# All sixteen gate chunks as split products, the recurrence's scan in four parts, attention outputs kept by ScalarE

## The chip, the cores and the metric

The kernel runs on one core of a Trainium2 chip. The metric is the device time of one launch in microseconds (us). Engines are named TensorE (PE; its weight loads are PEld), VectorE (DVE), ScalarE (ACT), GpSimd (POOL) and SyncE (SP, which issues most DMAs).

## What is computed

One inference step of a two-layer encoder, for 256 new prompt tokens and 32 sample tokens, 288 token columns in all, width 1024. The reference, cut to one layer:

```
z = x @ w_in                      # columns: [rnn 1024 | q 1024 | k 128 | v 128 | rnn gate 1024 | attn gate 1024]
q, k = rope(z_q), rope(z_k)       # 16 query heads, 2 key/value heads of 64
g_rnn, g_attn = sigmoid(z_gr), sigmoid(z_ga)
u  = causal depthwise conv (width 4) of z_rnn
gx = sigmoid(u @ w_x + b_x); ga = sigmoid(u @ w_a + b_a)      # 16 blocks of 64
a  = exp(-8 * ga * softplus(-a_param)); b = sqrt(1 - a*a) * gx * u
h_t = a_t * h_(t-1) + b_t                                     # the recurrence, over the tokens
o  = attention of q over its own and the two previous chunks of 64 tokens, with a sink per head
m  = g_rnn * (h @ w_br_rnn) + g_attn * (o @ w_br_attn)
x  = layernorm(alpha * x + m @ w_out)
x  = layernorm(alpha * x + shared_expert(x) + top-8-of-64 experts(x))
```

All data are float32.

## The kernel before, in words

Activations lie transposed, features on the 128 partitions and 288 tokens along the free axis (`xT`, eight chunks of 128 features). A weight matrix comes in **pieces** of 1024 x 256 (1 MB), one DMA each, into a ring of three slots (`dense`). The list `PIECES` gives their order: four for the rnn stream, one for k and v, four for q (`D_Q` = 5), eight for the gates (`D_G` = 9), eight for the two branches, four for `w_out`, and the rest. SyncE loads piece d when piece d-3 has been used.

A piece gives two output **chunks** of 128 columns, and TensorE makes a chunk in one of two ways:

- `over_features` (L569): eight plain float32 products, which the profile records as 16 MATMULs;
- `over_parts` (L582 to L584): weight and activation are each split into a high and a low part of type float32r, and three products (high x high, high x low, low x high) are made for each of eight feature chunks: 24 MATMULs. For this ScalarE copies the piece to its high part (`high_parts`, L1069, two instructions of 128x1024 for a piece) and VectorE subtracts to get the low part (`low_parts`, L1409, two instructions). The list `SPLIT` names the pieces that are split; a piece's place in it is called f here. The high part has two buffers, so piece f waits until piece f-2 has been used.

Each engine has its program written out by hand, and they wait for each other's semaphores only. The stretch that matters here is the attention stage of each layer. It has, on TensorE, in this order (L702 to L799): sixteen gate chunks in five places ahead of and between the attention steps, set by the tables

```
GATES_AHEAD = ((0, 1), (2, 3), (4,))
GATES_WITH = ((5, 6), (7,), (8,), (9, 10), (11,), (12, 13), (14,), (15,))
```

1. The projection of q: eight chunks, each followed by the two gate products of the recurrence (L695), whose sigmoids ScalarE writes (L1153), while VectorE rotates q (L1504 to L1507).
2. Gate chunk 0; two transposes of k (L722) and the 32 sample tokens' scores (L734, L735); gate chunk 1.
3. Transposes of the sample tokens' probabilities (L743, L744), which wait for VectorE to normalise them (L1534); scores of pair 0 (`pair_scores`, L713, L714); gate chunks 2 and 3.
4. Output of the sample tokens (L756, L757), which waits until ScalarE has copied the transposed probabilities (L1188, L1189; semaphore `s_pT_kept`); gate chunks 4, 5 and 6.
5. The loop over the eight **pairs** c of heads: scores of pair c+1, gate chunk(s) of `GATES_WITH[c]`, output of pair c-1 (`pair_output`, L771 to L773), transposes of pair c's probabilities (L791). Afterwards the output of pair 7, one transpose of the states (L799), and the branch products (L582 to L584 again).

Chunk m of the gates is written to bank m % 2 of PSUM, and ScalarE applies a tanh and keeps it (`keep_gates`, L1162); chunk m+2 waits for that. In `bank_of` gate chunk 0 waits until all of the recurrence's gate products in even banks have been read.

Beside this, VectorE has for pair c: `mask_and_max(c)` (L1562 to L1526: adds the mask to the scores, takes the row maxima) when the scores are there; `normalise` (L1531 to L1534) when ScalarE has made the exponentials (L1203); `keep_output` (L1587), a copy of the pair's output out of PSUM; and `low_parts` in the turns that `LOW_WITH` names. ScalarE has the exponentials, two copies of the transposed probabilities (L1224, L1225), the gates, and `high_parts` in the turns of `HIGH_WITH`.

The **recurrence** runs beside it: ScalarE computes the decay a (L1177, eight instructions) and a tanh (L1182, eight), VectorE computes the squares (L1553, L1554, four pairs), ScalarE a square root (L1193), and VectorE multiplies and scans all eight feature chunks in one block (L1573 to L1579), after `mask_and_max(0)` and ahead of `normalise` of pair 0. From the scan come a high part by ScalarE (L1214, at pair `H_WITH` = 2) and a low part by VectorE (L1598, L1599, one pair later).

After the attention stage come the branch products, `w_out`, a layer norm, the router, and sixteen rounds over four experts each. In the first of these, between the experts' first products (`up`, L910) and `turn` (L920), the shared expert's second product is made (`shared_down`, L871, eight chunks in two banks); VectorE adds each chunk to the residual (L1792), and TensorE waits for the last of these before it goes on. VectorE makes the one-hot table of the next four experts (`one_hot`, L1722) after them.

## Time and profile before

| | us |
|---|---|
| median of 3 runs | 1590.09 (1589.77 to 1591.45) |
| the profiled execution, its own time | 1589.3 |
| its span, first to last instruction | 1587.5 |
| TensorE busy | 1550.0 (98% of the span) |
| VectorE busy | 741.5 (47%) |
| ScalarE busy | 573.9 (36%) |
| attention stage of a layer (TensorE's gate chunk 0 to the transpose of the states) | 90.2 |

TensorE is busy in nearly all of the span, and the chain of work that ended last runs over it for 92% of the time. A busy share is an average: matmuls overlap, and inside the attention stage the three engines wait for each other for fractions of a microsecond. The two layers have the same timeline, shifted by 783.32 us; where the text reads a time of the second layer, the first layer's is that much earlier.

### The profile page before, as it was taken

The page shows a single profiled execution, that of the slowest core. Times are in us where ns is not written, and L with a number is a line of the kernel's source. Part 1 is how long each engine was busy: PE and PEld are TensorE (multiplying, and loading weights), DVE is VectorE, ACT ScalarE, POOL GpSimd, SP SyncE. Part 2 cuts the span into 40 slices and gives each one's busy share as a digit, 9 for nine tenths or more (in the row PEclk, how much of TensorE's full clock was granted, in tenths as well). Part 3 has the DMA queues.
Part 4 walks back from the last instruction along what each step waited for, and adds up shares of the span by engine and source line. Part 5 has one row for each costly group of instructions (what it writes and reads, how often), then busy time and mean ns, then how long its engine had stood idle before and what let it go on. Part 6 is the DMA issues. An engine that isn't in the chain of part 4 may idle for free.

```text
span 1587.5 us, 25312 instructions
## 1 busy us (share of the span) xinstructions
PE 1550.0 (98%) x9446; PEld 1034.5 (65%) x9446; DVE 741.5 (47%) x1513; ACT 573.9 (36%) x1108; POOL 25.0 (2%) x40
## 2 busy tenths in 40 slices
PE   7999999999999999999999999999999999999996
PEld 7968997655655565555598699975565555556554
DVE  5768667332433333233474776562243333324335
ACT  5756433222232232223267664342223223222322
POOL 2000000000000000000010000000000000000000
PEclk9999999999999999999999999999999999999998
DMA  8552446599999999999546424458999999999991
GB/s 235 188 209 85 134 160 245 212 372 409 410 399 402 401 417 401 403 404 402 206 127 232 153 91 153 147 212 322 401 404 398 408 404 416 400 404 407 401 407 45
DMA packets 141557, 477.38 MB, mean 301 GB/s; under 512 B 10020, under 2 KB 74084, under 8 KB 108724
## 3 DMA queue, kind: packets, MB, share of 16 engines
q1 hardware_dynamic: 139728, 473.50, 77.0%
q0 software_dynamic: 1408, 2.85, 0.7%
q8 instruction: 44, 0.72, 0.2%
q10 hardware_dynamic: 356, 0.13, 0.0%
q14 instruction: 21, 0.17, 0.0%
HBM read 474.88 MB, written 1.57 MB: 300 GB/s over the span
## 4 chain that ended last, share of the span: by engine, by line
PE 92%; DVE 5%; ACT 2%; issue 1%; DMA 0%; SPq 0%; DVEq 0%; ACTq 0%
PE ps L910 28%; PE ps L933 14%; PE ps L582 6%; PE ps L583 6%; PE ps L584 6%; PE ps L569 6%; PE ps L954 4%; PE ps L955 4%; PE ps L893 4%; PE ps L892 4%; PE ps L895 2%; PE ps L942 1%; PE ps L871 1%; PE ps L920 1%; PE ps L1004 1%
## 5 line engine op out<-in xcount | busy, mean ns | idle before, releaser
L910 PE MATMUL ps<-experts,xg 128*64 128x512 f32 x2048 | 445.0, 592 | 0.0
L910 PEld LDWEIGHTS ps<-experts,xg 128*64 128x64 f32 x2048 | 146.9, 137 | 291.5 <-issue 290.6
L582 PE MATMUL ps<-parts 128*128 128x288 f32 x768 | 232.4, 303 | 1.1 <-DVE dense_lo L1409 0.4
L933 PE MATMUL ps<-experts,hid 128*64 128x512 f32 x1024 | 226.8, 595 | 0.4 <-ACT hid L1283 0.4
L584 PE MATMUL ps<-parts,dense_lo 128*128 128x288 f32 x768 | 226.1, 294 | 0.0
L1749 DVE SCALAR_TENSOR_TENSOR yl<-ps,gsl,yh 128x512 fp32r<-128x512 f32 x128 | 96.1, 751 | 254.8 <-ACT yh L1291 254.8
L1737 DVE TENSOR_TENSOR hid<-ps,hid 128x256 f32<-128x256 f32 x64 | 27.2, 425 | 378.6 <-ACT hid L1278 378.6
L1278 ACT ACTIVATE hid<-ps 128x256 f32<-128x256 f32 x64 | 24.6, 385 | 404.8 <-PE ps L910 404.8
L933 PEld LDWEIGHTS ps<-experts,hid 128*64 128x64 f32 x1024 | 71.6, 137 | 131.9 <-issue 127.9
L1270 ACT ACTIVATE xg<-ps,gperm_all 128x256 f32<-128x256 f32 x256 | 130.8, 562 | 71.5 <-PE ps L895 71.5
L582 PEld LDWEIGHTS ps<-parts 128*128 128x128 f32 x768 | 144.3, 188 | 4.8 <-issue 2.3
L584 PEld LDWEIGHTS ps<-parts,dense_lo 128*128 128x128 f32 x768 | 144.5, 188 | 0.0
L892 PE MATMUL ps<-oh,xh 128*128 128x256 f32 x512 | 136.4, 288 | 0.0
L1291 ACT ACTIVATE yh<-ps,gsl 128x512 fp32r<-128x512 f32 x128 | 88.1, 688 | 128.8 <-PE ps L933 128.8
L893 PE MATMUL ps<-oh,xl 128*128 128x256 f32 x512 | 133.5, 282 | 0.0
L954 PE MATMUL ps<-ohT,yh 128*128 128x288 f32 x480 | 132.2, 305 | 0.0
L955 PE MATMUL ps<-ohT,yl 128*128 128x288 f32 x480 | 129.1, 295 | 0.0
L1409 DVE TENSOR_TENSOR dense_lo<-dense,parts 128x1024 fp32r<-128x1024 f32 x96 | 113.2, 1221 | 19.4 <-ACT parts L1069 19.4
L569 PE MATMUL ps<-xT,dense 128*128 128x288 f32 x448 | 112.6, 409 | 4.4 <-ACT B L1153 2.7
L1756 DVE TENSOR_TENSOR ffT<-ps,ffT 128x288 f32<-128x288 f32 x240 | 109.6, 456 | 15.4
L583 PE MATMUL ps<-parts 128*128 128x288 f32 x384 | 113.3, 295 | 0.0
L1069 ACT ACTIVATE parts<-dense 128x1024 fp32r<-128x1024 f32 x96 | 96.1, 1052 | 42.3 <-PE ps L584 41.7
(287 smaller groups left out, 1964.0 us busy)
## 6 DMA issues: line engine op xcount, KB each, us to landing
experts<-in_w SPq DMA_DIRECT2D x384, 1024.0 KB, 10.0
dense<-in_w_in SPq DMA_DIRECT2D x34, 1024.0 KB, 5.5
dense<-in_w_br_rnn SPq DMA_DIRECT2D x8, 1024.0 KB, 5.3
dense<-in_w_br_attn SPq DMA_DIRECT2D x8, 1024.0 KB, 5.2
dense<-in_w_out SPq DMA_DIRECT2D x8, 1024.0 KB, 5.2
dense<-in_ws SPq DMA_DIRECT2D x6, 1024.0 KB, 5.5
tok<-in_x_prompt SPq DMA_DIRECT2D x1, 1024.0 KB, 5.7
out_y_prompt<-tok SPq DMA_DIRECT2D x2, 512.0 KB, 2.6
```

The costliest lines, as they stand in the source:

```text
L569: last = mm(bank[:, 0:n], w[:, k, col:col + P], rhs(k), start=k == 0, stop=k == KC - 1)
L582: mm(bank[:, 0:T], w_hi[:, k, col:col + P], hi[:, k, :], start=k == 0, stop=False)
L583: mm(bank[:, 0:T], w_hi[:, k, col:col + P], lo[:, k, :], start=False, stop=False)
L584: last = mm(bank[:, 0:T], w_lo[:, k, col:col + P], hi[:, k, :], start=False, stop=k == KC - 1)
L892: mm(o, xh[:, t, x], oh[:, t, :], start=t == 0, stop=False)
L893: mm(o, xl[:, t, x], oh[:, t, :], start=False, stop=False)
L910: last = mm(ps[e % 2 * CAP:(e % 2 + 1) * CAP, UP[u], :], xg[:, k, e * CAP:e * CAP + CAP], experts[:, e, 0:2, k * DE:k * DE + DE], start=k ...
L933: last = mm(ps[e % 2 * CAP:(e % 2 + 1) * CAP, DOWN[u][b], :], hidT[:, u, m, e % 2 * CAP:(e % 2 + 1) * CAP], experts[:, e, 2, m * D + b * 5 ...
L954: mm(o, yh[:, u, c * P:c * P + P], ohT[:, u, :], start=u == 0, stop=False)
L955: last = mm(o, yl[:, u, c * P:c * P + P], ohT[:, u, :], start=False, stop=u == 1)
L1270: last = activation(xg[:, k, :], ps[:, SWAP[j], k % 2 * 256:k % 2 * 256 + 256], ACT.Identity, bias=gperm_all[:, L, 1, k:k + 1], scale=gper ...
L1409: V.tensor_tensor(low[:, x], slot[:, x], as_f(whi[:, f % 2, x]), ALU.subtract).then_inc(wlo_ready, 1)
```

## The change

- **Split.** The gate pieces that were not split (the first four, gate chunks 0 to 7) join `SPLIT`. Their high and low parts are made in two new turns of the q projection (after q chunks 5 and 7), and at two new places (`F_G - 2`, `F_G - 1`) between that and the pairs.
- **Order of the gates.** `GATES_AHEAD` becomes ((0, 1, 2), (3,), (4,)). ScalarE keeps chunk 0 ahead of the sample tokens' exponentials, chunk 1 behind them. Gate chunk 0 waits only for the read of the product that last used its bank. The last gate chunk, 15, is made in two halves of four feature chunks, one ahead of pair 6's output, one ahead of pair 7's.
- **Recurrence.** The multiply and scan are made for two feature chunks at a time: part 0 where the whole stood, parts 1 to 3 in the turns of pairs 0 to 2. The high part of h is made one pair later (`H_WITH` = 3), and so is the low part.
- **Outputs.** `keep_output` moves from VectorE to ScalarE.
- **Shared expert.** TensorE goes on with `turn` and the transposes of the gate table before it waits for VectorE's last addition, and VectorE makes the next one-hot table ahead of the additions.

```diff
-SPLIT = list(range(D_IN + 1, D_KV + 1)) + list(range(D_Q, D_G)) + list(range(D_G + 4, D_ROUTER))
+SPLIT = list(range(D_IN + 1, D_KV + 1)) + list(range(D_Q, D_ROUTER))
-GATES_AHEAD = ((0, 1), (2, 3), (4,))
+GATES_AHEAD = ((0, 1, 2), (3,), (4,))
-H_WITH = 2
+H_WITH = 3
...
-                elif i >= Z_GATE:
+                elif i == Z_GATE:
+
+                    pe.wait_ge(z_free[i % 2], z_count(L, Z_GATE - Z_GATE % Z_DEEP) + 1)
+                elif i > Z_GATE:
                     pe.wait_ge(z_free[i % 2], z_count(L, i))
...
+                def last_gate(ks):
+                    m = 2 * KC - 1
+                    if ks[0] == 0:
+                        bank_of(L, Z_GATE + m)
+                    return over_parts(L, ps[:, z_bank(Z_GATE + m), :], D_G + m // 2, m % 2 * P, x_hi, x_lo, ks=ks)
+
...
-                    if c > 0:
+                    if c == KC - 1:
+                        last_gate(range(KC // 2))
+                        pair_output(c - 1)
+                    elif c > 0:
...
+                last_gate(range(KC // 2, KC)).then_inc(z_ready[(2 * KC - 1) % 2], 1)
                 pair_output(KC - 1)
...
-                    if c in (1, 3):
+                    if c % 2:
                         high_parts(L, F_Q + 2 + c // 2)
...
+                act.wait_ge(xc_used, L + 1)
+                keep_gates(GATES_AHEAD[0][:1])
                 act.wait_ge(s_max, L * (KC + 1) + 1)
...
+                keep_gates(GATES_AHEAD[0][1:2])
+                high_parts(L, F_G - 2)
                 act.wait_ge(gxu, L + 1)
...
                 keep_gates(GATES_AHEAD[1])
+                high_parts(L, F_G - 1)
                 act.wait_ge(m2_ready, (L + 1) * (KC // 2))
...
+                def keep_output(c):
+                    act.wait_ge(s_o, L * (KC + 1) + c + 2)
+                    activation(qT[:, c, 0:TP], ps[:, 6, 0:TP], ACT.Copy).then_inc(o_ready, 1)
...
+                    if 0 < c < KC - 1:
+                        keep_gates(GATES_WITH[c])
                     if c > 0:
-                        keep_gates(GATES_WITH[c])
+                        keep_output(c - 1)
...
+                def recurrence(j):
+                    x, c = slice(2 * j * U, 2 * (j + 1) * U), slice(2 * j, 2 * j + 2)
+                    dve.wait_ge(mult_ready, L + 1)
+                    link(V.memset(gl_[:, c, 0:1], 1.0))
+                    V.memset(a_[:, c, 0:1], 0.0)
+                    V.memset(a_[:, c, US - 1:US], 0.0)
+                    link(V.tensor_tensor(gxF[:, x], gxF[:, x], glF[:, x], ALU.mult))
+                    link(V.tensor_copy(gx_[:, c, US - 1:US], h0[:, c, :]))
+                    V.tensor_tensor_scan(glF[:, x], aF[:, x], gxF[:, x], 0.0, ALU.mult, ALU.add).then_inc(h_scan, 1)
...
+                recurrence(0)
...
                     if c == 0:
                         mask_and_max(1)
-                    if c > 0:
-                        keep_output(c - 1)
+                    if c < 3:
+                        recurrence(c + 1)
+                    if c == 2:
+                        last_states()
                     if c in LOW_WITH:
                         low_parts(L, F_G + LOW_WITH.index(c))
...
                     slots_to_tokens(n, 1)
+                    if after:
+                        after()
...
                     hidden(q, 0)
                     hidden(q, 1)
+                    dve.wait_ge(og_ready, q + 1)
+                    one_hot(q + 1, 1)
```

Three places show the new order; line numbers in the rows of the change are its own. First, ScalarE from the last q chunk (rows `tmp<-ps`) to the copy of the sample tokens' probabilities (`PTa<-ps`), before:

```order
L1153 ACTIVATE B<-ps,prm_all 128x291 [waits z_free0,z_ready0]
L1153 ACTIVATE B<-ps,prm_all 128x291 [waits z_free1,z_ready1]
L1169 ACT_TABLE_LOAD
L1169 ACTIVATE S,ats<-ps,ats 128x160 [waits s_max]
L1169 ACTIVATE S,ats<-ps,ats 128x160 x3
L1171 ACTIVATE ats<-ats 128x4
L1177 ACTIVATE B<-B,c 128x291 [waits z_free1,decay_set,z_free0,gxu]
L1177 ACTIVATE B<-B,c 128x291 x7
L1162 ACTIVATE B<-ps 128x288 [waits z_ready0,xc_used]
L1162 ACTIVATE B<-ps 128x288 [waits z_ready1]
L1182 ACTIVATE B<-B,c 128x291 [waits act_own]
L1182 ACTIVATE B<-B,c 128x291 x7
L1188 ACTIVATE PTa<-ps 128x256 [waits s_pT]
```

and in the change:

```order
L1081 ACTIVATE parts<-dense 128x1024 [waits z_ready1,dense_in1]
L1081 ACTIVATE parts<-dense 128x1024
L1174 ACTIVATE B<-ps 128x288 [waits z_ready0,xc_used]
L1183 ACT_TABLE_LOAD
L1183 ACTIVATE S,ats<-ps,ats 128x160 [waits s_max]
L1183 ACTIVATE S,ats<-ps,ats 128x160 x3
L1185 ACTIVATE ats<-ats 128x4
L1174 ACTIVATE B<-ps 128x288 [waits z_ready1]
L1081 ACTIVATE parts<-dense 128x1024 [waits z_ready1,dense_in2]
L1081 ACTIVATE parts<-dense 128x1024
L1193 ACTIVATE B<-B,c 128x291 [waits z_free1,decay_set,z_free0,gxu]
L1193 ACTIVATE B<-B,c 128x291 x7
```

Two copies to a high part (`parts<-dense`, L1069 before and L1081 now, two instructions each) stand ahead of the decays and the tanhs, which are followed by the same copy to `PTa`.

Second, VectorE from the mask of pair 2 (`S<-ps,cst`) to the mask of pair 3, before:

```order
L1562 TENSOR_TENSOR S<-ps,cst 128x384 [waits s_pT,s_scores]
L1562 TENSOR_TENSOR S<-ps,cst 128x384
L1565 TENSOR_REDUCE ats<-S 128x2 [waits s_masked]
...
L1534 TENSOR_SCALAR S<-S,ats 128x128 x2
L1587 COPY qT<-ps 128x256 [waits s_o]
L1409 TENSOR_TENSOR dense_lo<-dense,parts 128x1024 [waits whi_ready] x2
L1562 TENSOR_TENSOR S<-ps,cst 128x384 [waits s_pT,s_scores]
```

and in the change:

```order
L1588 TENSOR_TENSOR S<-ps,cst 128x384 [waits s_pT,s_scores]
L1588 TENSOR_TENSOR S<-ps,cst 128x384
L1591 TENSOR_REDUCE ats<-S 128x2 [waits s_masked]
...
L1559 TENSOR_SCALAR S<-S,ats 128x128 x2
L1603 MEMSET B 128x2 [waits mult_ready]
L1604 MEMSET B 128x2 [waits dve_own]
L1605 MEMSET B 128x2
L1606 TENSOR_TENSOR B<-B 128x582
L1607 COPY B<-prm_all 128x2 [waits dve_own]
L1608 SCALAR_TENSOR_TENSOR B<-B 128x582 [waits dve_own]
L1434 TENSOR_TENSOR dense_lo<-dense,parts 128x1024 [waits whi_ready] x2
L1588 TENSOR_TENSOR S<-ps,cst 128x384 [waits s_pT,s_scores]
```

The copy out of PSUM is gone and a part of the recurrence (six instructions; its scan is the row `SCALAR_TENSOR_TENSOR B<-B 128x582`) stands ahead of the low parts.

Third, VectorE at the shared expert, from the experts' hidden values (`hid<-ps,hid`) on, in the change:

```order
L1765 TENSOR_TENSOR hid<-ps,hid 128x256 [waits silu_done]
L1746 ISA [waits og_ready]
L1750 TENSOR_TENSOR oh<-cst,rank 128x768 [waits xg_full]
L1822 SCALAR_TENSOR_TENSOR ffT<-xT,ps 128x288 [waits z_ready0]
L1822 SCALAR_TENSOR_TENSOR ffT<-xT,ps 128x288 [waits z_ready1]
```

The one-hot table (`oh`) stood behind the eight additions (`ffT<-xT,ps`, L1792 before) and now stands ahead of them.

## Rows read from the trace of the kernel before

**Rows 1.** TensorE's waits, second layer's attention stage: total us, times, longest

```profile
PE ps L569 <- ACT B L1153: 1.4, 1, 1.4
PE ps L743 <- DVE S L1534: 1.3, 1, 1.3
PE ps L771 <- ACT PTa L1225: 1.0, 1, 1.0
PE ps L569 <- ACT B L1162: 0.7, 1, 0.7
PE ps L791 <- DVE S L1534: 0.5, 1, 0.5
```

**Rows 2.** Chain in order of time, same stage: start us, us, what

```profile
887.58 0.36 PE ps L756 x2
...
890.46 11.84 PE ps L569 x48
902.30 0.64 PE ps L713 x4
...
923.28 0.33 PE ps L582
...
926.67 0.65 PE ps L791 x6
...
932.65 0.81 PE ps L791 x6
```

**Rows 3.** Branch products: us, busy (instructions) of PE PEld DVE ACT POOL, PEclk, DMA, GB/s

```profile
177.00:245.00 68.00, 68.00 (x516) 67.95 (x515) 42.15 (x62) 24.70 (x30) 3.00 (x5) 1.00 0.45 145
```

**Rows 4.** ScalarE, timeline, second layer: start us, us, instruction [idle before, releaser]

```profile
873.11 0.39 ACT L1169 ACTIVATE S<-ps,ats 128x160 f32<-128x160 f32 x1 [5.32 <-DVE ats L1526]
...
875.61 3.54 ACT L1177 ACTIVATE B<-B,c 128x291 f32<-128x291 f32 x8 [0.80 <-DVE B L1548]
...
879.63 3.53 ACT L1182 ACTIVATE B<-B,c 128x291 f32<-128x291 f32 x8
...
884.12 0.38 ACT L1162 ACTIVATE B<-ps 128x288 f32<-128x288 f32 x1
...
908.53 2.00 ACT L1069 ACTIVATE parts<-dense 128x1024 fp32r<-128x1024 f32 x2
```

**Rows 5.** VectorE, timeline, second layer's attention stage

```profile
891.56 0.07 DVE L1573 MEMSET B<- 128x8 f32 x1 [1.86 <-ACT B L1193]
...
894.51 5.01 DVE L1579 TENSOR_TENSOR_SCAN B<-B 128x2328 f32<-128x2328 f32 x1
...
903.22 1.02 DVE L1562 TENSOR_TENSOR S<-ps,cst 128x384 f32<-128x384 f32 x2 [1.76 <-PE ps L714]
...
905.81 1.02 DVE L1562 TENSOR_TENSOR S<-ps,cst 128x384 f32<-128x384 f32 x2
...
908.80 1.01 DVE L1534 TENSOR_SCALAR S<-S,ats 128x256 f32<-128x256 f32 x4
...
910.76 2.35 DVE L1409 TENSOR_TENSOR dense_lo<-dense,parts 128x1024 fp32r<-128x1024 f32 x2
...
922.12 2.28 DVE L1598 TENSOR_TENSOR h_lo<-B,parts 128x2048 fp32r<-128x2048 f32 x1
```

**Rows 6.** VectorE, timeline, first layer, q projection: the sinks' tables

```profile
76.94 1.38 DVE L1400 COPY sinkS<-sinkP 32x4 f32<-32x4 f32 x8
```

**Rows 7.** Chain in order of time, first layer, shared expert

```profile
299.80 7.97 PE ps L871 x32
...
308.49 0.65 PE ps L920 x4
```

**Rows 8.** VectorE, timeline, first layer, shared expert

```profile
308.43 0.96 DVE L1722 TENSOR_TENSOR oh<-cst,rank 128x768 fp32r<-128x768 f32 x1 [0.19 <-DVE ffT L1792]
```

**Rows 9.** Stretches at the end of the program, columns as in rows 3

```profile
1575.00:1577.00 2.00, 0.28 (x2) 0.00 (x0) 1.51 (x8) 1.08 (x3) 0.00 (x0) 1.00 0.00 0
1577.00:1578.00 1.00, 0.00 (x0) 0.00 (x0) 0.96 (x3) 1.00 (x2) 0.00 (x0) 0.80 0.00 0
```

More of the change, by code:

```diff
@@ L570, in over_features, with over_parts @@
                 return last
-            def over_parts(L, bank, d, col, hi, lo, ready=None):
+            def over_parts(L, bank, d, col, hi, lo, ready=None, ks=range(KC)):
                 f = SPLIT.index(d)
@@ L576, in over_parts @@
                 w_lo = dense_lo[:, d % RING, :].rearrange("p (k c) -> p k c", k=KC)
-                for k in range(KC):
+                for k in ks:
                     if col == 0 and k % 4 == 0:
@@ L872, in shared_down, with shared_added @@
                         last.then_inc(z_ready[c % 2], 1)
+                def shared_added():
                     for b in range(2):
@@ L956, in combine, with quad @@
                         last.then_inc(c_full, 1)
-                def quad(n, first=False, last=False):
+                def quad(n, first=False, last=False, after=None):
                     if not first:
@@ L976, in round_of @@
                         meanwhile()
-                    quad(q, first=True)
+                    quad(q, first=True, after=shared_added if meanwhile else None)
                     with pe.Fori(1, NQUAD - 1) as i:
@@ L1225, in _ @@
                     activation(PTa[:, w, 1, :], ps[:, 5, 0:3 * P], ACT.Copy).then_inc(s_pT_kept, 1)
+                    if c == KC - 1:
+                        keep_gates(GATES_WITH[c])
                     if c in HIGH_WITH:
                         high_parts(L, F_G + HIGH_WITH.index(c))
+                keep_output(KC - 1)
                 act.wait_ge(o_ready, (L + 1) * (KC + 1))
@@ L1514, in _ @@
                         sink_tables()
-                    if c in (1, 3):
+                    if c > 0 and c % 2:
                         low_parts(L, F_Q + 2 + c // 2)
@@ L1603, in _ @@
                         mask_and_max(1)
-                    if c > 0:
-                        keep_output(c - 1)
+                    if c < 3:
+                        recurrence(c + 1)
+                    if c == 2:
+                        last_states()
                     if c in LOW_WITH:
                         low_parts(L, F_G + LOW_WITH.index(c))
-                keep_output(KC - 1)
                 low_parts(L, F_BR + 1)
@@ L1756, in add_output, with quad @@
                         V.tensor_tensor(ffT[:, c, :], ps[:, SWAP[c % len(SWAP)], 0:T], ffT[:, c, :], ALU.add).then_inc(c_added, 1)
-                def quad(n, i, first=False, last=False, hidden_made=False):
-                    if not last:
+                def quad(n, i, first=False, last=False, made=False):
+                    if not last and not made:
                         dve.wait_ge(og_ready, n + 1)
                         one_hot(n + 1, i + 1)
-                    if not hidden_made:
+                    if not made:
                         hidden(n, 0)
@@ L1805, in round_of @@
                         meanwhile()
-                    quad(q, 0, first=True, hidden_made=first)
+                    quad(q, 0, first=True, made=first)
                     with dve.Fori(1, NQUAD - 1) as i:
```

31 lines of the change are left out of this document (9 added, 22 removed).

## Prediction

> **What bounds the kernel now.** I read the busy shares first: TensorE is busy for 98% of the span, VectorE for 47%, ScalarE for 36% (the table of the profile). That says only that TensorE's own work or a wait of TensorE has to shrink; whether the other two engines have room is a question of where, not of their average. The second view is TensorE's waits inside the attention stage, the one stage that the change rebuilds: 1.4, 1.3, 1.0, 0.7 and 0.5 us, all for ScalarE or VectorE [rows 1]. That is 4.9 us a layer. These are idle times from the modelled end of the last matmul; the next one could have started some 0.2 us before that end, so the first, second and fourth cost about 4.1 us together and not 3.4. The third view is the order of time around these waits, on TensorE [rows 2], ScalarE [rows 4] and VectorE [rows 5].
>
> I work in the second layer's times. The median of the runs is 1590.1 us, the profiled execution 1589.3 us; I sum against the latter and add the same difference to the median.
>
> **Gate chunks.** A plain chunk costs 11.84 / 3 = 3.95 us [rows 2]. A split chunk in a row of them costs 24 x 68.00 / 516 = 3.16 us [rows 3]; alone between other work, from its first product to the next kind, 926.67 - 923.28 = 3.39 us [rows 2]. Of the eight chunks that change, five stand first in their group and three behind another: 5 x 3.39 + 3 x 3.16 = 26.4 us against 31.6, a gain of 5.2 us a layer. Chunk 15 in two halves pays the 0.2 us of a start once more. If all old waits went too, a layer would win 5.2 - 0.2 + some 5.5. The price is 4 more high parts of 2.00 us on ScalarE [rows 4] and 4 more low parts of 2.35 us on VectorE [rows 5], and the recurrence in the midst of the pairs. The rest is about whether these are covered.
>
> **Up to the pairs: 5.4 us earlier.** ScalarE ended its q work at 866.5; a table load and 5.32 us of idle time followed, to 873.11 [rows 4]. The high part behind q chunk 5 lies in its idle time. The one behind q chunk 7 lasts until 868.5, VectorE's low part of its second half (1.2) until 869.7; two small copies later VectorE takes the sample scores, at 870.2, where it was 871.6, so the exponentials start at 871.7 instead of 873.1. They last 1.7 (873.11 to 875.61 less the wait of 0.80); keeping chunk 1 takes 0.4, the next high part 2.0: 875.8. Then decays 3.4, chunk 2 0.4, tanhs 3.4, copies of the probabilities 1.1: they are out at 884.2, which is where they are now (884.12 is the instruction behind them [rows 4]). The 1.4 us won ahead of the exponentials and the 0.8 us wait for VectorE are eaten by 2.0 us of high part.
>
> TensorE comes earlier. It reached the sample output at 887.58 [rows 2]. Without the three waits (4.1) and with chunks 0 to 3 split (15.8 becomes 13.3, so 2.5) it is there at 881.0. So **a wait of 3.2 us for ScalarE stands where none was**; the output starts at 884.2, 3.4 us earlier than before. Chunks 4 to 6 take 3.39 + 2 x 3.16 = 9.7 instead of 11.84 us. Call the start of pair 1's scores T: it was 902.3 and becomes 896.9.
>
> **The pairs: 5.5 us later.** VectorE's steps from row to row: a mask with its maxima 905.81 - 903.22 = 2.6; a normalisation 1.35 (1.01 and its two small predecessors); low parts 2.3, their first half 1.2; the recurrence's block lasted 899.52 - 891.56 = 7.96 us, so a quarter is 2.0, plus four instructions' fixed time and links again, 2.5 [rows 5]. The bounds of this last price are 2.0 (nothing fixed) and 2.7; I take 2.5, because every one of its six instructions is issued four times. The mask of pair 1 starts 0.9 us behind T. Then, in VectorE's order, recurrence 2.5, mask 2.6, normalisation 1.35, recurrence 2.5, first half of the low part for chunk 8 1.2: chunk 8 can start at T + 13.7. TensorE's own work up to there is short: a pair's turn with one chunk takes 932.65 - 926.67 = 6.0 us [rows 2], so it stands there at T + 8.7, and **waits 5.0 us** in two pieces, ahead of pair 1's transposes (about 2.4) and of chunk 8 (about 1.9), with 0.6 in small change. The second half of the low part, a mask and a normalisation end at T + 18.9, where TensorE is at T + 18.2: 0.7 more. With pair 3 there are two chunks in the turn and nothing waits. With pair 4 the low part of h (2.28 [rows 5] and a small second part, some 2.6) now falls into a turn with one chunk: mask, h, normalisation are 6.6 us behind the 0.9 of the scores, TensorE's own way 5.2: 2.3 more. Together 8.0 us. Off come the old waits of 0.5 and 1.0 and two small ones (2.0), chunk 7's 0.6, and on goes the half chunk's 0.2: plus 5.5 us.
>
> `keep_output` on ScalarE takes 0.35 us off VectorE per pair and adds 0.4 to ScalarE, whose turns have room; its cover is ScalarE's wait for the next maxima, and if it is gone it costs its 0.4 in each of eight turns. Only behind the last pair does it show: half chunk, high part, output and the high part of o now follow each other on ScalarE, and o's low part ends some 0.15 us after TensorE has finished the first two branch chunks; 0.15 a layer. DMAs keep their number; each gate piece is asked for when the piece three before it is used, at least 8 us ahead of its high part, so none is late.
>
> **First layer.** It has the sinks' tables on VectorE, 2 us, of which [rows 6] shows the longest part, just ahead of the first new low part. That makes the rotation of q chunk 6, the last sigmoids and all behind them later; I follow it through to T as 1.25 us.
>
> **Shared expert.** TensorE could go on 0.7 us earlier (307.77 to 308.49 [rows 7]), and another 0.25, as a product can follow ahead of the modelled end. But the one-hot table, 0.96 us [rows 8], now stands ahead of the additions that free the two banks, and holds the third chunk for 0.5: minus 0.45 a layer.
>
> **Sum.** Second layer -5.4 + 5.5 = +0.1; first +0.1 + 1.25 = +1.35; branches +0.3; shared -0.9: **+0.9 us**, 1590.2 for the execution profiled, **1591.0** as a median. Differences within 0.2% (3.2 us) are what a measurement of this kernel can't tell from none.
>
> **Rivals.**
>
> *The cover holds.* For it speaks that in the attention stage of 90 us ScalarE and VectorE are not full. If my VectorE chains are too long by half of each wait I found (11.2 us a layer, so 5.6), the time is about 1580; chance 0.19. If no wait is left, old or new, both layers give 10.5 and the shared expert 0.9: about 1569; chance 0.08. Against it: each engine's order is fixed, and the three waits of 3.2, 5.0 and 2.3 follow from rows added up.
>
> *The clock falls* (the slower side). No wait inside the kernel is longer than 1.4 us now, and the granted clock is 1.00 throughout. After the program's last matmuls (0.28 us of them in 1575 to 1577) it reads 0.80 in the microsecond from 1577 [rows 9], so in that microsecond it left its upper level of 2.4 GHz for 1.2 GHz, with TensorE idle. My forecast has TensorE idle for 3.2 us at one place and for 2.4 and 1.9 with little between them at another. Each fall costs between nothing and a whole chunk made at half speed (3.4); the middle, 1.7, once or twice in each layer, gives +3 to +6: 1594 to 1597. It decides if the level changes at one of these waits, with TensorE as the bound behind it. Chance 0.20. The Trainium skill ("TensorE: Matmul & The Clock Gate", Part 1: The HAM clock gate) says that the throttled state is the default and activity releases it; by that rule each new long wait is followed by slow products, +3 to +6 as above, and the trace agrees for the end of the program [rows 9].
>
> *ScalarE is later still.* Its chain from 866.5 to 884.2 has no slack left. If each high part ends 0.5 us later than I think, or the decays wait, T moves by 1 to 1.5 us in both layers: 1594. Chance 0.08.
>
> **Chances.** The forecast has 0.45, nearly all within 0.2%. Faster by more than 0.2%: 0.27 of the first rival and a little of the forecast's edge, 0.31 in all. Slower: the two others and the other edge, 0.31. Same: 0.38. The range takes in the half-covered case and the clock's: 1580 to 1597; the forecast's own is 1588 to 1594.
>
> **What would show it.** Right: no plain gate chunks, split chunks at 3.2 to 3.4 us; a wait of about 3 us of TensorE for the copies of the sample tokens' probabilities; waits of about 2 us for pair 1's normalisation, for chunk 8's low part and for pair 4's normalisation; the wait for the last sigmoid (1.4) gone. Wrong: if VectorE's recurrence parts lie in its idle time and chunk 8 does not wait, the first rival holds; if the granted clock is under 1.00 inside the attention stage, the second.

## The result

The change is slower: 1599.42 us (1599.16 to 1599.82) against 1589.93 us (1588.79 to 1591.45) for the kernel before on the same chip, ratio 1.0059, 95% interval 1.0043 to 1.0075. The forecast was 1591.0, the range ended at 1597. One execution of a later kernel (the change with eight chunks plain) took 1767.9 us at a mean granted clock of 0.847 and stands in none of the comparisons.

The head of the profile of the change:

```profile
span 1597.3 us, 25646 instructions
...
PE 1553.9 (97%) x9574; PEld 1049.7 (66%) x9574; DVE 757.1 (47%) x1549; ACT 593.1 (37%) x1140; POOL 24.9 (2%) x40
```

TensorE has more busy time than before (1550.0), although the 16 gate chunks that are now split, eight in each layer, should have saved it 10.4 us. TensorE's waits in the second layer's attention stage (total us, times, longest us) answer to [rows 1]:

```profile
PE ps L798 <- DVE S L1559: 4.6, 2, 2.4
PE ps L754 <- ACT PTa L1204: 3.0, 1, 3.0
PE ps L585 <- DVE dense_lo L1434: 0.8, 1, 0.8
PE ps L711 <- DVE S L1588: 0.3, 1, 0.3
```

The old waits are gone, and the four that I had forecast stand there: 3.0 us for the copies of the sample tokens' probabilities (3.2 forecast), two of at most 2.4 for the normalisations of pairs 1 and 4 (2.4 and 2.3), and one for chunk 8's low part, of 0.8 where I had 1.9. So far the forecast holds. The chain of waits in order of time, second layer, shows what doesn't (start us, us, what); it answers to [rows 2]:

```profile
887.48 0.26 ACT PTa L1203
887.75 0.27 ACT PTa L1204
888.02 0.14 issue
888.15 0.57 PE ps L754 x2
888.72 0.61 PE ps L755 x2
...
892.42 0.61 PE ps L755 x2
893.04 0.54 PE ps L585
893.58 0.24 PE ps L586
893.82 0.24 PE ps L587
...
898.14 0.24 PE ps L587
898.38 0.24 PE ps L585
898.75 0.14 PE ps L587
```

Two products of the sample tokens' output took 0.36 us before [rows 2] and take 0.61 here; a product of chunk 4 takes 0.24 us, from 898.75 on one takes 0.14. The granted clock in the same stretches (the columns are us; PE, PEld, DVE, ACT and POOL busy; PEclk, the granted clock; DMA share; GB/s):

```profile
884.00:888.00 4.00, 1.18 (x9) 0.95 (x8) 3.42 (x5) 4.00 (x12) 0.00 (x0) 1.00 0.34 93
888.00:892.00 4.00, 3.85 (x13) 1.90 (x14) 3.86 (x6) 3.97 (x6) 0.00 (x0) 0.53 1.08 400
892.00:896.00 4.00, 4.00 (x16) 3.34 (x16) 3.80 (x13) 2.94 (x2) 0.00 (x0) 0.50 0.74 295
896.00:900.00 4.00, 4.00 (x23) 4.00 (x23) 2.47 (x4) 1.08 (x4) 0.00 (x0) 0.69 0.01 3
...
912.00:916.00 4.00, 1.55 (x16) 1.31 (x15) 3.73 (x16) 3.60 (x12) 0.00 (x0) 0.94 0.80 241
916.00:920.00 4.00, 3.23 (x16) 2.47 (x15) 3.93 (x6) 3.18 (x6) 0.00 (x0) 0.50 0.07 21
...
940.00:944.00 4.00, 1.81 (x15) 1.24 (x10) 3.93 (x10) 1.27 (x7) 0.00 (x0) 0.86 0.76 261
944.00:948.00 4.00, 4.00 (x25) 3.62 (x25) 3.09 (x7) 2.77 (x4) 0.00 (x0) 0.72 0.00 1
```

0.50 is the lower of the clock's two levels, 1.2 of 2.4 GHz. In the 4 us that hold the long waits TensorE was busy for 1.18, 1.55 and 1.81 us, and the clock fell in them or at their end. In the first layer the sample output starts at 101.53 us, and the clock falls later, in the midst of it, with TensorE busy:

```profile
100.00:104.00 4.00, 2.47 (x13) 1.25 (x13) 3.83 (x6) 3.98 (x9) 0.00 (x0) 0.90 0.99 337
104.00:108.00 4.00, 4.00 (x16) 3.34 (x16) 3.93 (x6) 3.97 (x3) 0.00 (x0) 0.50 1.03 409
```

Before the change no stretch inside the kernel is under 1.00. Over the whole stages (the same columns, first and second layer):

```profile
80.00:178.00 98.00, 88.15 (x690) 78.72 (x689) 75.18 (x179) 66.47 (x171) 1.07 (x2) 0.93 0.39 131
...
858.00:957.00 99.00, 90.23 (x671) 81.04 (x670) 73.69 (x167) 66.17 (x165) 1.07 (x2) 0.90 0.43 147
```

A mean of 0.93 over 98 us is (1 - 0.93) x 98 / 0.5 = 14 us at the lower level, 0.90 over 99 us is 20 us: 34 us in all.

For the experiments I use two lengths (us) of each layer's attention stage, from TensorE's own starts in the profiled execution: A, from the recurrence's last gate products to pair 1's scores, and B, from there to the transpose of the states. "Falls" is the number of times that the granted clock fell there, in A + in B. First layer / second layer:

| kernel | A | B | falls |
|---|---|---|---|
| before | 38.8 / 38.8 | 54.0 / 54.0 | none |
| forecast (sum) | 34.6 / 33.4 | 59.5 / 59.5 | none |
| the change | 37.4 / 37.5 | 60.4 / 61.4 | 1+2 / 1+2 |
| all four waits filled | 34.5 / 33.1 | 58.9 / 58.8 | none |
| first wait filled | 34.5 / 34.6 | 60.4 / 60.4 | 0+1 / 1+1 |
| copies moved | 32.9 / 31.5 | 61.0 / 59.5 | 0+2 / none |
| recurrence together | 37.4 / 37.5 | 56.7 / 52.9 | 1+1 / 1+0 |
| change, eight chunks plain | 34.9 / 34.9 | 60.2 / 58.8 | 0+1 / none |
| rearranged | 32.9 / 31.5 | 52.9 / 53.0 | none |
| rearranged, eight chunks plain | 34.9 / 34.9 | 52.2 / 52.2 | none |
| two parts in pair 3's turn | 31.4 / 30.1 | 54.0 / 54.0 | none |
| spread | 31.4 / 30.1 | 51.9 / 51.9 | none |

### The profile page after: what moved, and what is told of

Read it like the earlier page. It is cut to its first block, busy times and chain, and to the rows that moved or that the text cites. A ratio compares the mean times of both kernels' runs of the same rounds, so it can differ in the third digit from the quotient of the medians.

```text
span 1597.3 us, 25646 instructions
## 1 busy us (share of the span) xinstructions
PE 1553.9 (97%) x9574; PEld 1049.7 (66%) x9574; DVE 757.1 (47%) x1549; ACT 593.1 (37%) x1140; POOL 24.9 (2%) x40
## 4 chain that ended last, share of the span: by engine, by line
PE 89%; DVE 6%; ACT 3%; issue 1%; DMA 0%; SPq 0%; DVEq 0%; ACTq 0%
PE ps L920 28%; PE ps L943 14%; PE ps L585 6%; PE ps L586 6%; PE ps L587 6%; PE ps L964 4%; PE ps L965 4%; PE ps L902 4%; PE ps L903 4%; PE ps L572 2%; PE ps L905 2%; PE ps L952 1%; PE ps L879 1%; PE ps L930 1%; DVE dense_lo L1434 1%
## 5 line engine op out<-in xcount | busy, mean ns | idle before, releaser
L585 PE MATMUL ps<-parts 128*128 128x288 f32 x896 | 275.3, 307 | 2.5 <-DVE dense_lo L1434 1.7
L587 PE MATMUL ps<-parts,dense_lo 128*128 128x288 f32 x896 | 266.6, 298 | 0.0
L585 PEld LDWEIGHTS ps<-parts 128*128 128x128 f32 x896 | 171.5, 191 | 8.3 <-issue 4.2
L587 PEld LDWEIGHTS ps<-parts,dense_lo 128*128 128x128 f32 x896 | 171.6, 192 | 0.0
L586 PE MATMUL ps<-parts 128*128 128x288 f32 x512 | 154.2, 301 | 0.0
L1434 DVE TENSOR_TENSOR dense_lo<-dense,parts 128x1024 fp32r<-128x1024 f32 x112 | 132.1, 1220 | 28.0 <-ACT parts L1081 27.9
L1081 ACT ACTIVATE parts<-dense 128x1024 fp32r<-128x1024 f32 x112 | 112.1, 1051 | 40.0 <-PE ps L587 39.7
L964 PEld LDWEIGHTS ps<-ohT,yh 128*128 128x128 f32 x480 | 90.2, 188 | 24.3 <-issue 24.3
```

The source lines that it names most:

```text
L585: mm(bank[:, 0:T], w_hi[:, k, col:col + P], hi[:, k, :], start=k == 0, stop=False)
L586: mm(bank[:, 0:T], w_hi[:, k, col:col + P], lo[:, k, :], start=False, stop=False)
L587: last = mm(bank[:, 0:T], w_lo[:, k, col:col + P], hi[:, k, :], start=False, stop=k == KC - 1)
L964: mm(o, yh[:, u, c * P:c * P + P], ohT[:, u, :], start=u == 0, stop=False)
L1081: activation(whi[:, f % 2, x], dense[:, d % RING, x], ACT.Copy).then_inc(whi_ready, 1)
L1434: V.tensor_tensor(low[:, x], slot[:, x], as_f(whi[:, f % 2, x]), ALU.subtract).then_inc(wlo_ready, 1)
```

## The experiments

Theory 1: the waits end where my sum put them, and what is over it is the clock, falling behind three of them in each layer. Theory 2, its rival: the waits and the chains of ScalarE and VectorE behind them cost the time themselves, and slow products only fill time that would have been idle. The eleven kernels ran in three sets; beside each set the kernel before had a median of 1590.04, 1589.47 and 1589.52 us.

Medians hold one thing more than A and B. The first 32 records of plain products in the program (timeline of TensorE: start us, us; first the kernel before, then the change with all waits filled) take

```profile
12.19 8.00 PE L569 MATMUL ps<-xT,dense 128*128 128x288 f32 x32 [0.16 <-ACT xT L1059]
12.16 9.82 PE L572 MATMUL ps<-xT,dense 128*128 128x288 f32 x32
```

8.00 us in six of the thirteen profiles and 9.7 to 10.4 us in the other seven, because the first seven to ten of them start 0.48 us apart instead of 0.24. This lies ahead of everything that the change touches, and it moves an execution by some 2 us. So where medians of a few executions differ by 2 us or less, the lengths of the profiles' stages decide.

### The waits filled with products

```diff
+            def fill_wait(n):
+                for _ in range(n):
+                    mm(ps[:, 7, 256:512], ident, cst[:, 0:256], start=True, stop=True)
...
+                fill_wait(6)
                 pe.wait_ge(s_pT_kept, L * (KC + 1) + 1)
...
+                    if c in (1, 4):
+                        fill_wait(5)
                     pe.wait_ge(s_norm, n + 1)
```

and `fill_wait(3)` ahead of chunk 8.

> The change, with products that nothing reads put on TensorE ahead of its long waits: six ahead of the sample tokens' output, five ahead of the transposes of pairs 1 and 4, three ahead of gate chunk 8. Theory 1 (the clock): the profile of the change shows the granted clock at 0.50 to 0.53 in 888 to 896 and at 0.50 in 916 to 920, each time behind a wait of 2 to 3 us; with TensorE occupied in these waits the granted clock stays at 1.00 in the attention stages, the waits keep their ends, and the time falls from 1599.4 to about 1591 (1590 to 1593), which is what my sum gave without the clock. Theory 2 (the waits alone): the time is set by the chains of ScalarE and VectorE, the slow products only fill idle time; then it stays at 1598 to 1600, or gets longer by what the extra products overrun.

1588.07 us (1587.2 to 1590.88), ratio 0.9987 [0.9978, 0.9995]: 11.35 us less than the change, by adding work, and 2 us under the band that I had given. A and B together are 11.5 us shorter; the two profiled executions differ by 9.3 us only, as the start of the program took 2.2 us longer in this one. TensorE at the first wait, timeline, second layer:

```profile
882.70 2.75 PE L642 MATMUL ps<-cst 128*128 128x256 f32 x12
885.84 0.40 PE L760 MATMUL ps<-PTa,vc_all 128*64 128x128 f32 x2 [0.39 <-ACT PTa L1214]
```

and the stretches from there, and around pair 1's transposes:

```profile
884.00:888.00 4.00, 3.61 (x20) 2.10 (x18) 3.83 (x6) 3.98 (x10) 0.00 (x0) 1.00 0.96 313
888.00:892.00 4.00, 4.00 (x30) 3.66 (x30) 3.93 (x6) 3.97 (x3) 0.00 (x0) 1.00 1.03 410
...
908.00:912.00 4.00, 3.66 (x23) 2.43 (x21) 3.87 (x11) 4.00 (x13) 0.00 (x0) 1.00 0.39 134
912.00:916.00 4.00, 3.83 (x30) 3.69 (x32) 3.83 (x11) 0.56 (x2) 0.00 (x0) 1.00 0.02 4
```

Six products that nothing reads (twelve records) last 2.75 us, and the output starts when ScalarE is done, as without them: 19.75 us behind the last gate product here, 19.74 in the change. The clock stays at 1.00 in both stages. Theory 2 is out: the waits end where they did, and the time fell with the clock's falls.

One wait filled alone, `fill_wait(6)` ahead of the sample tokens' output:

> The change with products that nothing reads in one of the long waits alone: six ahead of the sample tokens' output. From the profiles of the change and of the run with all four places filled: up to pair 1's scores these differ by 2.9 us in the first layer and 4.4 in the second, from there to the transpose of the states by 1.5 and 2.6. If each fall of the clock has its own price, this run keeps the first saving and not the second: 1599.4 - 7.3 = 1592.1, with the granted clock still at 0.50 behind the waits of pairs 1 and 4. If a fall kept away early only lets TensorE run into a longer wait later, it stays over 1596.

1592.94 us (1592.24 to 1594.81), ratio 1.0023 [1.0013, 1.0033], against 1592.1 expected: a wait later in the stage does not take the saving back. That the number meets so closely is in part luck, for the falls were not the expected ones. Behind pair 1's wait of 2.4 us the clock did not fall in either layer (B is 60.4 in both, 1.0 less than in the change's second layer), and in the second layer it fell in spite of the filling (stretches as above):

```profile
884.00:888.00 4.00, 3.62 (x20) 1.89 (x18) 3.83 (x6) 3.98 (x9) 0.00 (x0) 1.00 1.04 368
888.00:892.00 4.00, 4.00 (x20) 3.96 (x19) 3.97 (x6) 3.96 (x3) 0.00 (x0) 0.57 1.01 401
```

It is a short fall, and A is 34.6 there for 33.1 with none. So six products do not keep the clock in every execution; why here and not in the run before is open.

### One move on ScalarE, and what a fall costs

ScalarE's four copies of the sample tokens' probabilities are put ahead of its eight tanhs:

```diff
-                act.wait_ge(act_own, (L + 1) * KC)
-                for c in range(KC):
-                    activation(gl_[:, c, :], gl_[:, c, :], ACT.Tanh, scale=c8[:, 1, L, c:c + 1]).then_inc(a_and_t, 1)
                 act.wait_ge(s_pT, L * (KC + 1) + 1)
...
                 last.then_inc(s_pT_kept, 1)
+                act.wait_ge(act_own, (L + 1) * KC)
+                for c in range(KC):
+                    activation(gl_[:, c, :], gl_[:, c, :], ACT.Tanh, scale=c8[:, 1, L, c:c + 1]).then_inc(a_and_t, 1)
```

> The change with one thing moved: ScalarE copies the sample tokens' probabilities (1.1 us) ahead of the eight tanhs (3.55 us) instead of behind them. The wait of 3 us ahead of the sample tokens' output goes, and with it the first fall of the clock; pair 1's scores come some 7 us earlier. The tanhs, the squares, the square root and the scan end 1.1 us later than now, so pair 0's transposes wait about 2 us for their normalisation and pairs 1 and 4 wait as long as in the change or longer, and the clock falls there: 1588 to 1593. If the waits in the pairs grow by all that is won ahead of them: 1597 or more.

1590.56 us (1588.86 to 1592.3), ratio 1.0003 [0.9994, 1.0012], in the middle of the band; A is 4.5 and 6.0 us shorter than in the change where I had expected some 7. Its two layers have the same waits ahead of the transposes, and the clock fell in the first layer only. TensorE at pair 1's transposes and at chunk 8, timeline, first layer:

```profile
125.79 1.54 PE L798 MATMUL ps<-cst,S 128*128 128x128 f32 x6 [2.44 <-DVE S L1559]
129.44 0.37 PE L585 MATMUL ps<-parts 128*128 128x288 f32 x1 [0.52 <-DVE dense_lo L1434]
```

and the granted clock there:

```profile
122.00:126.00 4.00, 1.49 (x14) 1.12 (x14) 3.72 (x17) 3.60 (x10) 0.00 (x0) 0.93 0.66 193
126.00:130.00 4.00, 3.48 (x18) 2.73 (x18) 3.93 (x5) 3.59 (x9) 0.00 (x0) 0.64 0.20 69
```

and second layer:

```profile
908.43 0.87 PE L798 MATMUL ps<-cst,S 128*128 128x128 f32 x6 [2.45 <-DVE S L1559]
912.08 0.37 PE L585 MATMUL ps<-parts 128*128 128x288 f32 x1 [1.92 <-DVE dense_lo L1434]
```

and its clock:

```profile
905.00:909.00 4.00, 1.55 (x17) 1.31 (x17) 3.72 (x16) 3.60 (x12) 0.00 (x0) 1.00 0.75 233
909.00:913.00 4.00, 2.08 (x18) 1.73 (x17) 3.93 (x6) 3.24 (x7) 0.00 (x0) 1.00 0.09 29
```

Two things are to be read here. The same wait of 2.44 us is followed by the lower level in one layer and by the upper in the other. And this fall costs nothing: chunk 8 starts 3.65 us behind the first transpose in both layers, since the slow transposes (1.54 us for 0.87) only shorten the next wait from 1.92 to 0.52. The first layer's second fall, at pair 4, has no wait behind it, and B is 61.0 against 59.5 there: 1.5 us. The same price stands in two other lines of the table, 60.4 against 58.8 (one fall in B, first wait filled) and 60.2 against 58.8 (eight chunks plain).

### The recurrence in one piece again

```diff
-                recurrence(0)
+                for j in range(4):
+                    recurrence(j)
+                last_states()
...
-                    if c < 3:
-                        recurrence(c + 1)
-                    if c == 2:
-                        last_states()
```

and `H_WITH` = 2.

> The change with the recurrence in one piece again (its four parts behind each other where part 0 stands, h's parts one pair earlier); all gate chunks stay split. VectorE is idle from 902.5 to 906 in the profile of the change and free in the pairs' turns then. Theory 1: the waits of 2.4 us at pairs 1 and 4 go and with them the second and third fall of the clock, the first stays: some 6 to 7 us less in each layer, 1585 to 1588. Rival: the scan in one piece delays pair 0's normalisation and so its transposes by what it wins later: 1597 to 1601.

1588.95 us (1587.15 to 1590.71), ratio 0.9989 [0.998, 0.9997]: a little over the band, 10.5 us under the change. In the second layer B falls to 52.9, with one wait of 1.4 us left for pair 0's normalisation and no fall. In the first layer, whose chain is later by the sinks' tables, that wait is 2.87 us, and the clock does fall (timeline of TensorE):

```profile
124.10 1.54 PE L798 MATMUL ps<-cst,S 128*128 128x128 f32 x6 [2.87 <-DVE S L1559]
```

So the rival's mechanism (pair 0 delayed) is there, but even with the clock it costs B 2.7 us in the first layer (56.7 for 54.0 before) and gains 1 in the second; the four parts of the change cost 6.4 and 7.4. The recurrence in one piece together with the moved copies was not run.

### Was it the split?

The first eight gate chunks are made as plain products again, in the change:

```diff
-SPLIT = list(range(D_IN + 1, D_KV + 1)) + list(range(D_Q, D_ROUTER))
+SPLIT = list(range(D_IN + 1, D_KV + 1)) + list(range(D_Q, D_G)) + list(range(D_G + 4, D_ROUTER))
...
-                high_parts(L, F_G - 2)
...
-                high_parts(L, F_G - 1)
```

> The change with the first eight gate chunks as plain products and without their four pieces' parts. ScalarE's chain to the sample tokens' probabilities is 2.0 us shorter, TensorE's way there 2.5 us longer: that wait and its fall of the clock go. The waits of the pairs stay, since the recurrence's parts do. Second layer: up to pair 1's scores 34.7 us (before 38.8, now 37.5), from there to the transpose of the states 54.0 + 5.5 + 0.6 = 60.1; so +2.1 against before, +3 in the first; less 1.1 at the shared expert: 1594. If the split was what cost the time: back to 1590 or less. If it carried its 5.2 us a layer in the change: 1603 or more.

1593.55 us (1591.2 to 1597.76, eleven executions), ratio 1.0028 [1.0018, 1.0037]: 1594 was expected. So the rest of the change loses time without any split: A is 3.9 us shorter in each layer than before, B 6.3 and 4.9 longer. The split in that order loses 5.9 us more. In the stages of the profiles it is 7.9: 5.2 in A, by the first wait that the split makes and the clock behind it, and 2.8 in B, nearly all in the second layer, where the clock fell twice instead of not at all. Its waits of 1.9 and 2.2 us at pairs 1 and 4 had one fall in the first layer, none in the second; the executions with a mean granted clock of 0.992 and 0.993 took 1597.1 to 1597.8 us, those at 0.995 and 0.996 1591.2 to 1594.1.

### The shared expert alone

The kernel before with the two edits at the shared expert:

```diff
+                def shared_added():
                     for b in range(2):
                         pe.wait_ge(z_free[b], z_count(L, Z_SH2 + KC))
...
                     slots_to_tokens(n, 1)
+                    if after:
+                        after()
...
                     hidden(q, 1)
+                    dve.wait_ge(og_ready, q + 1)
+                    one_hot(q + 1, 1)
```

> The kernel before with the change's part at the shared expert alone. By my sum minus 0.45 us a layer, so 0.9 us in all: 1589.0. If the wait was hidden anyway: no change, 1589.9. The profile of the change (from the shared expert's products to the end of the program) lets me expect 1.1 to 1.2.

1588.51 us (1587.24 to 1592.06), ratio 0.9991 [0.9982, 0.9999]. TensorE, chain in order of time, first layer:

```profile
299.50 2.14 PE ps L871 x8
301.68 6.09 PE ps L871 x24
307.76 0.44 PE ps L922 x4
```

The transposes follow the last product at once, where 0.7 us of wait stood [rows 7]. From the first product to the transposes it is 8.26 us for 8.69, my 0.45; from one layer's shared expert to the next layer's, and from the second to the end of the program, the profiles differ by 0.54 and 0.57 us, 1.1 in all. The medians differ by 1.5.

### The same work in another order

If theory 1 holds, the order of ScalarE and VectorE decides, not their load. TensorE's order is untouched; ScalarE's copies stand ahead of the tanhs, pair 0's mask ahead of the squares, and:

```diff
-H_WITH = 3
+H_WITH = 4
...
-                    if c == 0:
-                        mask_and_max(1)
-                    if c < 3:
-                        recurrence(c + 1)
-                    if c == 2:
+                    if c in (0, 2, 3):
+                        recurrence(max(c, 1))
+                    if c == 0:
+                        mask_and_max(1)
+                    if c == 3:
                         last_states()
```

> The change with the same work in another order on the two other engines, TensorE's order untouched: ScalarE copies the sample tokens' probabilities ahead of its eight tanhs instead of behind them; VectorE masks pair 0 ahead of the squares; the recurrence's part 1 stands ahead of pair 1's mask, part 2 in pair 2's turn, part 3 in pair 3's; the parts of h are made in pairs 4 and 5, where TensorE has two gate chunks. Theory 1 and the cover together: the output of the sample tokens need not wait (ScalarE can be done at 884.4, TensorE comes at 885.05 in the second layer), the waits of 2.4 us of pairs 1 and 4 shrink under 1 us, the clock stays at 1.00, and the time is 1569 to 1575. If the waits go and the clock is not what made them dear, half of that gain is left: 1584 to 1590. If the engines' total work binds and not its place, the waits only move: 1591 to 1599.

1572.65 us (1572.45 to 1575.69), ratio 0.9886 [0.9872, 0.99]: 26.8 us under the change with the same instructions, 17.4 under before. The clock's share of this is what the filling gave back, 11.35 us; the other 15 are waits that the new order does without (against the filled run A is 1.6 us shorter in each layer, B 5.9). TensorE's waits, second layer:

```profile
PE ps L711 <- DVE S L1582: 1.5, 1, 1.5
PE ps L585 <- ACT B L1174: 1.2, 1, 1.2
```

Behind these the clock stays at 1.00. The same kernel with plain chunks 0 to 7:

> The rearranged kernel (1572.65 us) with the first eight gate chunks made as plain products, as in the kernel before, and without the four pieces' high and low parts. My price for the split was 5.2 us a layer. In the rearranged kernel 1.5 and 1.3 us of wait a layer stand behind ScalarE and VectorE, which longer chunks would cover, so of the 5.2 some 2.5 to 3 are left to lose: 1578. If the split carries its full price: 1583. If the new order alone made the kernel faster and the split nothing: 1573.

1577.66 us (1576.29 to 1580.12), ratio 0.9925 [0.9913, 0.9938]; it has no wait over 0.3 us. The split is worth 5.0 us here (3.8 in A and B of the profiles), of the 10.4 that its products save; the two waits above, 2.7 to 2.8 us a layer, are about the rest. They were the next to go, by chunk 4 ahead of the sample tokens' output and other turns for the recurrence's parts:

```diff
-GATES_AHEAD = ((0, 1, 2), (3,), (4,))
+GATES_AHEAD = ((0, 1, 2), (3, 4), ())
...
-                    if c in (0, 2, 3):
-                        recurrence(max(c, 1))
                     if c == 0:
                         mask_and_max(1)
+                    if c == 2:
+                        recurrence(1)
                     if c == 3:
+                        recurrence(2)
+                        recurrence(3)
                         last_states()
```

> The rearranged kernel with two more moves: gate chunk 4 ahead of the sample tokens' output, so that it is kept before the square root and chunk 6 need not wait for its bank (1.3 us a layer now); and the recurrence's part 1 in pair 2's turn, parts 2 and 3 in pair 3's, so that pair 1's mask starts at once (wait of 1.5 us now, of which about 1.0 comes back ahead of pair 1's transposes, since two masks and a normalisation last 6.5 us where TensorE has 5.8 us of work). Minus 1.8 us a layer: 1569. If VectorE is late elsewhere for it: 1573 or more.

A median of 1577.44 us and not 1569, ratio 0.9918 [0.9905, 0.9932]. The five executions lie apart: 1572.1 at a mean granted clock of 0.997, 1574.7 and 1577.4 to 1577.7 at 0.995 and 0.996. The miss is my own: with two parts in one turn pair 4's normalisation comes late. TensorE's waits for it, second layer:

```profile
PE ps L798 <- DVE S L1559: 2.4, 2, 2.1
```

The profile is of the execution of 1572.1 us and has no fall; that the others had some is read from their mean clock alone. I filled that wait:

```diff
+                    if c == 4:
+                        fill_wait(4)
                     pe.wait_ge(s_norm, n + 1)
```

> The kernel with two recurrence parts in pair 3's turn, and four products that nothing reads in its one wait of 2.1 us, ahead of pair 4's transposes. If the spread of its executions (1572.1 to 1577.7) is the clock, falling at that wait in some of them: all are at 0.997 or more, median 1571 to 1573. If the spread has another cause, it stays: median 1575 to 1578.

1572.98 us (1571.94 to 1574.82), ratio 0.989 [0.9876, 0.9904], all four executions at 0.997 or 0.998. The upper group is gone, and so is the lower mean clock, though the transposes start when they did (B is 54.0 in both). What stays of the spread, some 3 us, most kernels here have, the one before too (1588.5 to 1592.5); the start of the program, 8.0 or some 10 us for its first 32 records, is 2 of them.

Last, the wait taken away instead of filled:

```diff
-H_WITH = 4
+H_WITH = 6
...
-                    if c == H_WITH + 1:
...
-                    if c == 2:
-                        recurrence(1)
-                    if c == 3:
-                        recurrence(2)
-                        recurrence(3)
-                        last_states()
+                    if c in (2, 3):
+                        recurrence(c - 1)
                     if c in LOW_WITH:
                         low_parts(L, F_G + LOW_WITH.index(c))
+                    if c == 5:
+                        recurrence(3)
+                        last_states()
+                    if c == H_WITH:
```

The low part of h moves with its condition, from ahead of the normalisation to the end of the turn.

> The rearranged kernel with gate chunk 4 ahead of the sample tokens' output, as in the run before this, and the recurrence's parts 1, 2 and 3 in the turns of pairs 2, 3 and 5; the high and the low part of h in pair 6's turn. In the run before (two parts in pair 3's turn) TensorE waited 2.1 us ahead of pair 4's transposes, and its executions went from 1572.1 at a mean granted clock of 0.997 to 1577.7 at 0.995 and 0.996. Without that wait: no wait over 1.2 us, every execution at 0.997 or more, 1569 to 1571. If VectorE is late elsewhere (pair 6 or 7, or h_ready ahead of the branches): 1572 to 1576.

1569.57 us (1568.1 to 1570.3), ratio 0.9867 [0.9853, 0.9882], all executions at 0.997. The only wait over 0.2 us that is left in the second layer's stage:

```profile
PE ps L798 <- DVE S L1559: 0.3, 1, 0.3
```

This is the fastest version, 20 us under the kernel before and 30 under the change. It is where the first rival's second case (all covered, about 1569) lay, and by its stages too: A and B are 9.5 and 10.7 us shorter than before, where the rival had 10.5 in each layer.

## Why the prediction was wrong

**What failed is one step of the sum: it took every matmul at the upper level of the clock.** I had written that mechanism down as the rival "the clock falls", gave it 0.20 and priced it at 3 to 6 us. It came, and cost 11.4. The runs part its size:

- *Where.* I saw two candidates (3.2 us, and 2.4 with 1.9 behind it) and passed over the third, pair 4's 2.3 us. The clock fell at all three, in both layers.
- *How long.* I took at most one chunk at half speed. In the second layer the clock was low for the whole sample output (4.9 us for 2.9) and for nearly all of chunk 4: 37.5 - 33.1 = 4.4 us. In the first layer, where the clock fell in the midst of the output (3.7 us for 2.9), it was 37.4 - 34.5 = 2.9.
- *What the next wait takes back.* B loses 1.5 us in the first layer, which is pair 4's fall alone: pair 1's costs nothing. In the second it loses 2.6, since pair 1's fall lasts longer there than the next wait can hide. Together 2.9 + 4.4 + 1.5 + 2.6 = 11.4 us, and filling the waits gave back 11.35 in the medians. Half of the 34 us at the lower level would be 17. The runs name two reasons for the difference: products in a row take 0.24 us for 0.135, not twice as long, and part of the delay goes into the next wait, as behind pair 1. How the 5.6 us divide between them is not measured.

The Trainium skill ("TensorE: Matmul & The Clock Gate", Terms) gives the penalty as about the throttled time times the share of pulses withheld. By that rule an estimate is 17 us here; the runs show 11.4, so in this kernel the rule gives too much. Part 1 of the page also says that the chip's observation is free-running and not tied to the kernel's start. The two layers of the run with the copies moved fit this, with one wait of 2.44 us and two outcomes, but no run here shows it to be the reason.

**Point by point, against the run with all waits filled:**

- *Split chunks, 5.2 us a layer.* The price of the products is right: chunks 4 to 6 take 9.8 us for 9.7, one alone 3.4. *Up to the pairs, 5.4 us earlier.* Right too: A fell by 5.65 us in the second layer and by 4.25 in the first (4.15 with the sinks' tables). But the split is a small part of that. With eight chunks plain A is 34.9 us, so the split is worth 0.4 and 1.8 us of A even with all waits filled; its wait for ScalarE takes most of the rest.
- *ScalarE done at 884.2, TensorE there at 881.0.* Right. From the last gate products that is 20.7 and 17.5 us; in the change the last copy ends at 20.3, and TensorE waits from 17.5 on.
- *Pairs 5.5 us later.* 4.9. A quarter of the recurrence takes 2.4 us on VectorE (908.81 to 911.22 in the change) for 2.5; the scan alone 1.37 us for a quarter where the whole took 5.01 [rows 5]. The waits of pairs 1 and 4 were sized right (2.4 and 2.2 us), and chunk 8's too: 1.92 us wherever the clock stayed up behind pair 1's.
- *First layer +1.25.* A differs by 1.3 to 1.4 us between the layers in every kernel with all gates split and no fall in A.
- *Branches +0.15 a layer.* Not there: from the transpose of the states to the router both kernels take 87.3 us.
- *Shared expert -0.45 a layer.* -0.55 in the kernel that has it alone.

Without the clock the forecast's 1591.0 would have met 1588.07, with its own range of 1588 to 1594: 2.9 us too high, by the pairs (1.2), the branches (0.3), A (0.35) and the shared expert (0.2), all on the same side; the rest is within the spread of the start. **The rival "the cover holds"** fell for the order that the change has, and came true for another order of the same work. I had argued against it that "each engine's order is fixed"; that was right, and it was the thing to change.

The chances: 0.31 on slower, with 0.20 on the clock, was too little. The trace of before had no wait over 1.4 us, and I forecast 3.2, 2.4 and 2.3 in each layer. With six such waits the question was how many would be followed by the lower level, not whether one would.

## What to carry to other kernels

When a change puts a new wait of two microseconds or more into a TensorE-bound stretch, price it twice: the wait, and the products behind it at half speed, until the next wait takes the rest back. Fill such a wait with products that nothing reads as a test, since it separates the two prices in one run. Then look for the order in which it does not arise: here four copies, 1.1 us together, ahead of 3.5 us of tanhs, pair 0's mask ahead of the squares, a gate chunk made earlier, and parts of the recurrence in turns with room turned a loss of 9.5 us into a gain of 20.

## What the hardware showed that I had not expected

- Waits of 2.2 to 3.1 us sufficed for the granted clock to fall, sometimes: the two of 2.97 and 3.08 us at the sample output each time in the profiled executions that had them, those of 2.2 and 2.4 in the pairs in some layers and not in others, those of 2.1 not in the one profile that has them. Behind waits of at most 1.9 us it fell in no profile, but for the filled one.
- The level also changed while TensorE was busy again: in the first layer of the change it fell within the sample output, more than 1 us behind the wait's end, and in the second layer chunk 4 ran for more than 5 us at 0.24 us a product before it was at 0.14.
- The level that the first products of the program find is not the same in every execution: 32 records took 8.0 us or 9.7 to 10.4.
- Six plain products were enough in one run and not in one layer of another (34.6 for 33.1 us of A), so filling is a test and a half measure; with the waits removed every execution of the fastest version was at 0.997.
- A fall need not cost anything: the time that slow transposes took, 1.54 us for 0.87, vanished in the next wait.
